# Projection steps of 24 products made as two steps of 12 in a planned TensorE order

## The reference, cut to what matters

```
def mixer_layer(x, pos, S0, k_past, v_past, buf, n_past, norm_pre, w_in, ...):
    h = rmsnorm(x, norm_pre)
    p = h @ w_in                                   # 1024 -> 3840, the input projection
    rq, rk, rv, rg, sq, sk, sv, sg, ca, cb, cg = jnp.split(p, idx, axis=-1)
    o_r, S = retention(rope(heads(rq), pos), rope(heads(rk), pos) * HEAD_DIM ** -0.5, heads(rv), S0)
    o_r = head_groupnorm(o_r, ret_gn_w) * jax.nn.silu(rg)
    o_s = stickbreak(heads(sq), k_all, v_all, sb_bias, n_past).reshape(B, T, SB_WIDTH) * jax.nn.silu(sg)
    o_c, buf_new = conv_module(ca, cb, buf, dw_w, dw_b, ln_w, ln_b, pw_w)
    o_c = o_c * jax.nn.silu(cg)
    y = jnp.concatenate([o_r, o_s, o_c], axis=-1) @ w_out    # the output projection
    return x + rmsnorm(y, norm_post), S, sk_h, sv_h, buf_new
```

## Time and profile before

| what | us |
|---|---|
| median of 3 runs | 1452.54 (1452.2 to 1453.28) |
| the profiled execution | 1451.64 |
| its span, first to last instruction | 1449.8 |
| TensorE matmul busy (8328 instructions) | 1382.0 |
| VectorE busy | 891.5 |
| ScalarE (ACT) busy | 764.6 |
| GpSimd (POOL) busy | 530.4 |
| mean granted TensorE clock | 0.983 of 2.4 GHz |

### The profile page before, as it was taken

One profiled execution on the slowest core, in us unless ns is written; L12 is line 12 of the kernel. 1 busy time (PEld: TensorE's weight loads), 2 busy tenths in 40 slices (PEclk: granted clock), 3 DMA queues, 4 the chain that ended last, 5 costly groups with the idle time before them and its releaser, 6 DMA issues.

```text
span 1449.8 us, 22660 instructions
## 1 busy us (share of the span) xinstructions
PE 1382.0 (95%) x8328; PEld 1176.3 (81%) x8328; DVE 891.5 (61%) x1378; ACT 764.6 (53%) x1517; POOL 530.4 (37%) x446
## 2 busy tenths in 40 slices
PE   6999899999999999999999999998999999999996
PEld 4888678778778878899978886886767888789995
DVE  2528998985542455476762398999745235545665
ACT  4555442476435555576645644336754364656642
POOL 1535531444423453131234454234343145431211
PEclk9999999999999999999999999999999999999998
DMA  6212004111023110535342110231111311015353
GB/s 230 73 60 74 20 19 128 59 51 38 15 78 109 54 35 16 164 133 186 120 144 74 44 49 16 63 99 64 36 34 45 98 65 54 16 59 194 130 172 109
DMA packets 81167, 116.99 MB, mean 81 GB/s; under 512 B 17442, under 2 KB 62882, under 8 KB 80930
## 3 DMA queue, kind: packets, MB, share of 16 engines
q1 hardware_dynamic: 65794, 59.98, 13.2%
q10 hardware_dynamic: 15264, 55.58, 11.5%
HBM read 89.81 MB, written 19.23 MB: 75 GB/s over the span
## 4 chain that ended last, share of the span: by engine, by line
PE 74%; DVE 16%; issue 4%; ACT 3%; POOL 1%; DMA 0%; SPq 0%; ACTq 0%; DVEq 0%
PE ring L1051 17%; PE ring L1053 16%; PE ring L1052 16%; DVE MX L1709 6%; PE AV L1202 3%; DVE MX L1710 3%; PE Z L1166 3%; PE Z L1266 2%; DVE MX L1806 2%; PE Z L1182 1%; DVE stop_lo L1584 1%; PE ring L1088 1%; PE ring L1074 1%; PE Z L1196 1%; PE Z L1180 1%
## 5 line engine op out<-in xcount | busy, mean ns | idle before, releaser
L1051 PE MATMUL ring<-H_hi,w_hi 128*128 128x352 f32 x1824 | 608.1, 333 | 13.4 <-DVE H_lo L899 5.4
L1053 PE MATMUL ring<-H_hi,w_lo 128*128 128x352 f32 x1824 | 587.6, 322 | 0.0
L1052 PE MATMUL ring<-H_lo,w_hi 128*128 128x352 f32 x1824 | 586.9, 322 | 0.0
L1051 PEld LDWEIGHTS ring<-H_hi,w_hi 128*128 128x128 f32 x1824 | 343.5, 188 | 49.4 <-issue 21.1
L1052 PEld LDWEIGHTS ring<-H_lo,w_hi 128*128 128x128 f32 x1824 | 344.4, 189 | 4.3
L1053 PEld LDWEIGHTS ring<-H_hi,w_lo 128*128 128x128 f32 x1824 | 343.6, 188 | 0.0
L908 POOL TENSOR_TENSOR w_lo<-w_raw,w_hi 128x1024 fp32r<-128x1024 f32 x58 | 149.5, 2577 | 306.4 <-ACT w_hi L1292 306.4
L1890 POOL TENSOR_SCALAR attend<-attend 128x512 f32<-128x512 f32 (+4 forms) x144 | 180.4, 1271 | 112.8 <-ACT attend L1361 112.8
L1577 DVE SCALAR_TENSOR_TENSOR attend<-Z,vec_sb,attend 128x512 f32<-128x512 f32 (+4 forms) x144 | 84.8, 613 | 138.4 <-ACT attend L1369 137.4
L1709 DVE SCALAR_TENSOR_TENSOR MX<-MX,vec_sb 128x1023 f32<-128x1023 f32 (+14 forms) x120 | 165.6, 1380 | 2.2
L1292 ACT ACTIVATE w_hi<-w_raw 128x1024 fp32r<-128x1024 f32 x82 | 86.6, 1056 | 69.2 <-PE ring L1053 43.6
(11 more groups left out here) (164 smaller groups left out, 1901.5 us busy)
## 6 DMA issues: line engine op xcount, KB each, us to landing
w_raw<-in_w ACTq DMA_DIRECT2D x81, 512.0 KB, 3.5
state<-in_w ACTq DMA_DIRECT2D x25, 512.0 KB, 3.5
out_yT<-MX SPq DMA_DIRECT2D x12, 704.0 KB, 4.3
swapped<-raw_rot SPq DMA_DIRECT2D x144, 44.0 KB, 1.9
attend<-in_cache_k SPq DMA_DIRECT2D x96, 64.0 KB, 1.9
attend<-in_cache_v SPq DMA_DIRECT2D x96, 64.0 KB, 2.2
attend<-in_xT SPq DMA_DIRECT2D x3, 1408.0 KB, 12.4
attend<-out_yT SPq DMA_DIRECT2D x3, 1408.0 KB, 12.6
```

Source lines behind the costliest of these rows:

```text
L1051: nc.tensor.matmul(in_ring(step), a, x, start=(n_k == 0), stop=False)
L1052: nc.tensor.matmul(in_ring(step), a, y, start=False, stop=False)
L1053: last = nc.tensor.matmul(in_ring(step), b, x, start=False, stop=(n_k == KB - 1))
```

## The change

A projection step becomes two steps in the planner and in TensorE's list. `("lead", i, c)` has the first four blocks of the contraction (12 products), claims the ring's bank and waits for the weights; `("proj", i, c)` has the other 12 and marks `s_full`. Both cost 1.93 us in the plan; the second follows the first, and other TensorE steps may be placed between them, ring jobs too. The second half has rank 2 where the step had and the lead has 3 (for the input blocks from the third on; 0 for the first two blocks, and 1 for output blocks, as before). The ring counts a projection at its lead, and holds its bank until the reader of the whole step is done. The planner is run anew, so the lists of all engines are new.

```
@@ Plan.order()
-        ring_kinds = ("proj", "vtok", "att", "ro", "ds9", "gn_mean", "gn_var", "ln_mean", "ln_var", "pw")
+        ring_kinds = ("lead", "vtok", "att", "ro", "ds9", "gn_mean", "gn_var", "ln_mean", "ln_var", "pw")
...
-                    job_of_bank[jobs % RING] = self.drain[step]
+                    job_of_bank[jobs % RING] = self.drain[("proj", *step[1:]) if step[0] == "lead" else step]
@@ plan(), the input projection
-            last = g.add("PE", step, 3.86, last, first, first2, low_of(base + i) if c == 0 else None, rank=3 if i >= 2 else 0,
+            last = g.add("PE", ("lead", base + i, c), 1.93, last, first, first2, low_of(base + i) if c == 0 else None, rank=3 if i >= 2 else 0,
                          lag=-1.5 if i == 0 else 0.0)
+            last = g.add("PE", step, 1.93, last, rank=2 if i >= 2 else 0)
@@ plan(), the output projection
-                last = g.add("PE", step, 3.86, last, low_of(i), *los, rank=1)
+                last = g.add("PE", ("lead", i, c), 1.93, last, low_of(i), *los, rank=1)
+                last = g.add("PE", step, 1.93, last, rank=1)
@@ build(), the ring's jobs
-            if step[0] in ("proj", "vtok", "att", "ro", "ds9", "gn_mean", "gn_var", "ln_mean", "ln_var"):
+            if step[0] == "lead":
+                jobs[("proj", *step[1:])] = len(jobs)
+            if step[0] in ("vtok", "att", "ro", "ds9", "gn_mean", "gn_var", "ln_mean", "ln_var"):
                 jobs[step] = len(jobs)
@@ build(), TensorE's block
-                elif kind == "proj":
+                elif kind in ("lead", "proj"):
                     i, c = step[1:]
                     l, n = divmod(i, LOADS)
                     out = n >= NB
-                    claim(step)
-                    if c == 0 or out:
-                        wait_weights(pe, i)
+                    step = ("proj", i, c)
+                    if kind == "lead":
+                        claim(step)
+                        if c == 0 or out:
+                            wait_weights(pe, i)
                     ks = OUT_K if out else list(range(KB))
-                    for n_k, k in enumerate(ks):
+                    for n_k, k in list(enumerate(ks))[0 if kind == "lead" else KB // 2:KB // 2 if kind == "lead" else KB]:
...
-                    last.then_inc(s_full.sem, s_full.mark(step))
+                    if kind == "proj":
+                        last.then_inc(s_full.sem, s_full.mark(step))
```

## The result

| | before | after |
|---|---|---|
| median of the runs, us | 1452.39 (1452.20 to 1453.28) | 1494.83 (1493.35 to 1496.23) |
| ratio | 1 | 1.0291, 95% interval 1.0273 to 1.0309 |
| the profiled execution, us | 1451.64 | 1493.35 |
| its span, us | 1449.8 | 1491.6 |
| mean granted clock, of 2.4 GHz | 0.983 | 0.979 |

The changed kernel is 2.9% slower. The prediction had 1462 us and a range up to 1484: the sign is right, the size is not.

The account below looks back on a forecast made before the run. The prediction took TensorE's work, and in parts of each layer VectorE, to bound the kernel. Its terms, -5 + 9 + 6 = +10 us, gave about 1462 us, with a range of 1436 to 1484.

Parts of the forecast that it names:

- steps which stay together cost 0: Projection: a lead directly followed by its second half is the same instruction stream as before, so it costs 0.
- the plan would go around most of the ring's waits: Ring banks: the plan counts the banks, so it would avoid most waits behind a parted step.
- only placed anew: DMAs and weight splits: the same jobs with the same due times, newly placed; no cost was given.
- Term 2: TensorE's interruptions of the projection: more pieces stand apart, adding edges; +9 us, bounds 0 and 36.
- Term 3: Projection steps ahead of waiting pieces: halved steps give less cover for VectorE's lateness; +6 us, bounds -20.3 and +18.
- What bounds it: Whole kernel: TensorE's work, busy 1382.0 of 1449.8 us, and for parts of each layer VectorE.
- Term 1: TensorE's idle time between start-up and tail, 39.4 us: finer steps fill some; gain of 5 us, bounds 0 and 39.4.
- the row that was to show the term right: Projection's first-line products: their mean rises by 3 ns or more over the third line's, showing more entries.
- the test that was given for it: Stop's second product: a wait for `stop_lo` below 12 us would mean Term 3 has the wrong sign.
- this rounding is what hides VectorE's lateness now: Projection: ready pieces wait for the running step's end, mean cover about 1.96 us; halved steps leave 0.98.
- The ring: Rival: a parted step holds one of three banks, so a third ring piece waits; 18 us, 1480 us, chance 0.10.
- The rival "faster": TensorE's idle time: half-steps before late stops, or earlier stops, fill half of 39.4 us; 1441 us, chance 0.32.

Follow-up runs that it names:

- e5: Changed kernel with state store planned before old x loads, no ring job between a half's two steps, no 0.25 us plan gap: 1446.94 us, ratio to before 0.9976.
- e13: The kernel of e5 run again on another chip: 1447.95 us, ratio to before 0.9976.
- e12: As e5, but only the weighing may stand between the two steps of a half (44 of 228 parted): 1446.08 us, ratio to before 0.9967.
- e7: Changed kernel, but no TensorE step may stand between a half's two steps (0 of 228 parted), plan gap kept: 1462.99 us, ratio to before 1.0082.
- e8: Changed kernel with the edits of e1 and e2 together, plan gap kept: 1453.99 us, ratio to before 1.0009.
- e2: Changed kernel with no ring job placed between the two steps of a half: 1467.44 us, ratio to before 1.0107.
- e1: Changed kernel with the retention state's store planned ahead of the old x loads on SyncE: 1476.41 us, ratio to before 1.0174.

## Why the prediction was right or wrong

Three steps failed: that steps which stay together cost 0, that the plan would go around most of the ring's waits, and that DMAs "only placed anew" need no term. Terms 2 and 3 together were to cost 15 us, and didn't.

**What bounds it** (TensorE's work, with its waits named by the view of waits): right. The new idle time is the new waits, 36.2 against 36.4 us.

**Term 1, idle filled, -5.** Wrong for this kernel: idle time in the middle grew, in the 1400 us between 50 and 1450 to 1400 - 1323.5 = 76.5 us, from 39.4. In e5 it is 1350 - 1313.0 = 37.0 in the stretch 50 to 1400 (37.1 in e13), 2.4 less than before. So it is small, half of the 5, and was covered up here by the ring and the store.

**Term 2, more edges, +9.** The entries came, the net did not. The rows of the two projection lines in after:

```profile
L1057 PE MATMUL ring<-H_hi,w_hi 128*128 128x352 f32 x1824 | 623.5, 342 | 13.8 <-DVE H_lo L903 9.8 <-POOL H_lo L903 1.8 <-DVE MX L1654 1.2
L1059 PE MATMUL ring<-H_hi,w_lo 128*128 128x352 f32 x1824 | 593.2, 325 | 0.0
```

342 - 325 = 17 ns against 11, 6 ns more, so the row that was to show the term right is there: 30.3 - 20.5 = 9.8 us more at the entries. But TensorE's whole busy time rose by only 5.6 in after, part of it at the lower clock behind the store's wait, and didn't rise in e5, e13 and e12, where the same difference stands 8.7, 9.0 and 6.0 us above before's. What failed is the reading of the price: the start-to-start distance at the two sides of an edge was summed as if it came on top of the pieces' own time. In the timeline above, the first product after L1117 has a bar of 0.72 us (from 586.49), but 0.56 of it lie under the bar of L1117 (585.95 to 587.05); in the earlier trace rows, the 0.24 us behind L1103 lie under L1103's bar, which ends at 223.92. So the difference of the two lines counts time that is the piece's too; how much of it is no cost at all, no run measured.

Nor does the difference give a price per edge. Against an unparted order with the same gap (before, or e7 with its 24.3 us) it is 0.14 us for each parted half in e12, 0.10 in e5, 0.05 in after and 0.04 in e8. The Trainium skill ("TensorEngine Tiling (Array Packing)", Key Properties) has TensorE drained at a change of the tiling mode, which the weighing's 128*64 is. With that, e12, parted by weighings alone, would agree, but e8, parted mostly by weighings and by scores (64*128), doesn't show it, and e12 as a whole is 0.33% below before.

**Term 3, less cover, +6.** The sign is wrong, by the test that was given for it: the wait for `stop_lo` fell from 20.3 to 4.7 us, under the 12 named. Part of that fall only moved to the first product of the stop: with the wait for `stop_hi` the sum is 22.8 before and 16.0 in after. In e12, e5 and e8, which hardly wait for `stop_hi` (1.8 us in e8, no row in the others), the wait for `stop_lo` is 10.5, 13.4 and 6.6. The step that failed: "this rounding is what hides VectorE's lateness now". Nothing parted and the same gap give 20.9 (e7), ring jobs barred 6.6 (e8): finer steps do help here.

**Steps that stay together, put at 0.** "A lead directly followed by its second half is the same instruction stream as before, so steps that stay together cost 0" is true of TensorE's stream, but not of the plan that orders the other engines: the 0.25 us between the two steps make each half 4.11 us long in it. e7 parts nothing and is 12 us slower than before.

**The ring, put at 0.10.** Its mechanism was right: "the third ring piece must then wait until the second half is done and drained" is the timeline at 590.14, and 18 jobs at 1 us were priced where 21 waits of 15.0 us went away with the ring jobs inside (e2). That all of the step from e1 to e8, 22.4 us, lies near the 18 is in part luck: bank waits are some 12 of it, and 9.5 are the wait for `stop_hi`, which the prediction didn't have. What failed is the step "the plan does count the banks, and would go around most of them". It counts them, but takes at each turn the step that can start first, and doesn't see that a job placed now makes a later one wait for the second half. So the case that came, though not alone, was the one that had a tenth. (The view also had more bank waits before than the "4.1 us in two": 5.7 in 8.)

**The store, not named at all.** 18.4 us. "the DMAs, the weight splits and their due times are the same jobs, only placed anew" is in the prediction as a cost of nothing; it was the place to ask which queue's order is held only by chance. A store's place in SyncE's list was worth more than any term of the sum. The rows to read were there before: a store, the loads 4.45 us behind it, and a weight load of ACT into the same tile.

With the ring at 18 and the store at 18, and Terms 1 to 3 near zero, the sum would have been 1452.5 + 36 = 1488, still 6 us short; the gap's 12 and the 9 that parting for attention pieces gave back are in none of its terms. The ring's 1480 is 4 us from e1 by luck: 10 of it are the Terms 1 to 3 that didn't come.

**The rival "faster"** (1441) is what remains when both are taken out, in part: 1446.1 to 1447.9. Its condition, that the order puts half-steps in front of late stops, is in line with the `stop_lo` waits of e5, e8 and e12.

## What to carry over

When a planner is given finer steps, first ask which of them hold a resource between their parts (a bank, a queue slot), and bar other users of that resource from the middle: here it was worth 22 to 33 us in three pairs of kernels, more than twice the 10 us that had been forecast for the whole change. Then compare the order of every queue before and after, above all DMAs that no dependency orders: a store that came behind two or three long loads cost 13 to 22 us at the far end of a chain over ACT and VectorE. And a change that is planned anew should be compared with a plan of the old steps at the new costs (e7: 12 us with nothing changed but a gap of 0.25 us in the plan).

## What the runs showed of the hardware

In this kernel the time until a store let go of its waiter depended on the loads issued ahead of it. The 512 KB store, whose median from issue to landing is 2.7 us before and 4.5 in after, held ACT for some 9.9 us after its issue when two loads of 1408 KB each (median 11.1 us) had been issued from 3.3 us before it on; with the store first (e1), ACT went on after 3.3 us. And ACT's wait for it, ahead of a DMA issue of 0.33 us, held back a copy of 0.46 us that had nothing to do with either.

After the 9.20 us of idle that this gave TensorE, its granted clock was 0.50 of 2.4 GHz from 606.89 to 610.93, and 0.96 from 611.59 to 613.86.
